# Branch steps ahead of the weight unit on ScalarE and VectorE in the token mixers of a two-layer encoder

## The chip, the cores and the metric

The kernel runs on one core of one Trainium2 chip. The metric is the device time of one execution in microseconds (us). The kernel before was timed three times; the figure that stands for it is the median, 1176.68 us.

## What is computed

The reference is a hybrid encoder trunk with two layers over 256 tokens of width 1024. Cut to what matters here:

```python
for l in range(DEPTH):                      # 2 layers
    xn = rms_norm(h, norm_mix_g[l])
    q, k, v, u_f, u_x, u_g, gates = split(xn @ w_in[l] + b_in[l])   # 1024 x 6144
    y_a = neighbourhood_attention(q, k, v, rpb[l])       # 8 heads of 64
    y_b = fourier_mix(u_f)                               # real part of a 2-D DFT
    y_c = recurrent_branch(u_x, u_g, ...)                # conv, forward and backward RG-LRU, GeLU gate
    merged = sum(sigmoid(gates_k) * (y_k @ w_branch[l, k]) for k in (a, b, c))
    h = h + merged @ w_out[l]
    xn = rms_norm(h, norm_ffn_g[l])
    h = h + (swiglu(xn, ...) if l % 2 == 0 else moe_swiglu(xn, ...))  # dense, then top-2 of 8 experts
return rms_norm(h, final_g)
```

All matrix products with weights are done to float32 accuracy: each operand is split into a high part in fp32r and the rest, and three products (high x high, high x rest, rest x high) are added up.

## The kernel before

Weights come as **units** of 128 x 1024 floats (512 KB). One unit passes through four hands. SyncE's queue loads it into a ring of six raw buffers (`load`, line 289). ScalarE copies it to its high part (`hi`, line 456), VectorE takes the difference (`lo`, line 758), and TensorE multiplies with both (lines 1245 to 1247). The split halves live in a ring of RH = 4 buffers, so ScalarE and VectorE work AHEAD = 3 units ahead: in turn k of a mixer they prepare unit k + 3 while TensorE is at unit k. `hi` of unit u waits until the load has landed and until TensorE has used unit u - 4, which is the moment TensorE begins turn u - 3. `lo` waits for `hi`; TensorE waits for `lo`; a load waits for the `lo` that frees its raw buffer.

A mixer has U_MIX = 68 turns: 48 for the input projection (12 groups of four units, in the order u_f, u_x, q, k, v, u_g and six for the gates), 12 for the branch projections and 8 for the output projection. The order of work on each engine is written out by hand: a loop over k with, in each turn, the branch steps due in it. TensorE does its small branch matmuls at the head of a turn, then the unit's 24 matmuls of 256 columns, or 12 of 512.

The steps that matter below, with the turn in which they stand:

- Turn 4 and 5 of layer 0: VectorE `set_up_columns` (lines 798 to 806, signals `col_ok`), ScalarE takes an absolute value and an exponential from it (lines 499 and 500, signal `lam_act`), VectorE `set_up_decay` (lines 812 to 825).
- Every fourth turn: the group that has just ended is evacuated from PSUM (lines 512, 518, 524 on ScalarE; 854, 860, 867 on VectorE).
- Turn 8: first Fourier matmuls (1332), copies (531, 894). Turns 9 to 12: the four taps of the convolution (883, 885). Turn 12: second Fourier matmuls (1341), copies and the mirror (902 to 910, signal `yb_full`). Turn 13: ScalarE makes the high part of y_b (535, `yb_h`). Turn 14: VectorE its low part (914, `yb_l`).
- Turn 16 and 25: TensorE's gate matmuls of the forward and the backward scan (1358). The first of them waits for `yb_l`. Activations 545, 555, 563, 571 and VectorE's 953 to 974 follow through turns 16 to 33; the scans are 971 and 974.
- Turns 28 to 48, every even one: attention, two heads on 128 queries at a time, j = 0 to 7. TensorE makes scores (1374; it waits for the row maximum of j - 1), the product with V of j - 3 (1386; it waits for `pt_ok`, and at each new pair of heads for `ya_l`) and transposes of j - 2 (1397). VectorE adds the bias and finds the maximum (930 to 933, `s_max`) and normalises j - 1 (937, 939). ScalarE copies the transposes (585) and takes the exponential (590). `ya_h` (596) and `ya_l` (945) split an output.
- Turns 34 to 41: the GeLU gate (981 to 995; 574, 577 on ScalarE).

GpSimd only adds the column mask to the attention's bias tables (418), four times in a mixer, as the tables land.

Of the kernel before, what the change touches and what calls it, by code (L numbers as in the profile page):

```python
# [42 lines left out]
AHEAD = RH - 1  # L43
# [9 lines left out]
U_MIX = U_IN + U_BR + U_OUT  # L53
# [50 lines left out]
def build(nc, x, norm_mix_g, w_in, b_in, rpb, conv_w, conv_b, lru_wa, lru_ba, lru_wx, lru_bx,  # L104
# [12 lines left out]
    with ExitStack() as ctx:  # L117
# [150 lines left out]
        def place(u):  # L268

            if u < BASE_MOE:  # L270
                return raw[:, u % RAW, :], raw_full[u % RAW], 16 * (u // RAW + 1)
            turn, j = (u - BASE_MOE) // RAW_MOE, (u - BASE_MOE) % RAW_MOE
            if j < RAW:
                return raw[:, (BASE_MOE + j) % RAW, :], raw_full[(BASE_MOE + j) % RAW], 16 * ((BASE_MOE + j) // RAW + turn + 1)
            return mix[:, UNIT * (j - RAW):UNIT * (j - RAW + 1)], mix_full[j - RAW], 16 * (turn + 1)
# [164 lines left out]
        def _(act):  # L440
# [7 lines left out]
            def hi(base, k, i=0, per=0):  # L448

                u = base + k  # L450
                ring = RAW_MOE if u >= BASE_MOE else RAW
                src, arrived, count = place(u)
                act.wait_ge(arrived, 16 * (per // ring) * i + count)
                if u >= RH:
                    act.wait_ge(unit_used, i * per + (u - RH + 1))
                act.activation(w_hi[:, u % RH, :], src, ACT.Copy).then_inc(hi_done, 1)  # L456
# [22 lines left out]
            def mixer(l):  # L479
                B = BASE_MIX[l]  # L480
# [10 lines left out]
                    norm(2 * l)  # L491
                    norm_hi(2 * l)
                for k in range(U_MIX):
                    if k + AHEAD < U_MIX:
                        hi(B, k + AHEAD)
                    if l == 0 and k == 4:

                        act.wait_ge(col_ok, 1)
# [98 lines left out]
                    for dg in range(2):  # L597
                        if k == U_IN + 6 * (dg + 1) + 1:
                            for b in range(2):
                                act.wait_ge(merged, 4 * l + 2 * dg + b + 1)  # L600
                                at = 1024 * dg + 512 * b
                                act.activation(xhf[:, at:at + 512], gflat[:, at:at + 512],
                                               ACT.Copy, scale=0.5).then_inc(mh_ok, 1)

            def step_hi(n, dst, i=0, per=0):

                for b in range(2):
                    act.wait_ge(prod_ok, 2 * i * per + (2 * n - 1 + b))
                    act.activation(dst[:, 512 * b:512 * b + 512], prod_t[:, 512 * b:512 * b + 512],
                                   ACT.Copy).then_inc(ah_ok, 1)  # L610
# [33 lines left out]
            def experts(p):  # L644
# [85 lines left out]
                rows_hi((E + 1) * (p + 1), 0)  # L730

            mixer(0)
            dense()
            mixer(1)
            norm(3)
            experts(0)
# [8 lines left out]
        def _(dve):  # L745
# [8 lines left out]
            def lo(base, k, i=0, per=0):  # L754

                u = base + k
                dve.wait_ge(hi_done, i * per + (u + 1))
                dve.tensor_tensor(w_lo[:, u % RH, :], place(u)[0],  # L758
                                  w_hi[:, u % RH, :].bitcast(F32), ALU.subtract).then_inc(lo_done, 1)
# [67 lines left out]
            def mixer(l):  # L827
                B = BASE_MIX[l]
# [5 lines left out]
                if l == 0:  # L834
                    lo(B, 2)
                for k in range(U_MIX):
                    if k + AHEAD < U_MIX:
                        lo(B, k + AHEAD)
                    if l == 0 and k == 4:
                        set_up_columns()  # L840
                    if l == 0 and k == 5:
# [180 lines left out]
                    for dg in range(2):  # L1022
                        if k == U_IN + 6 * (dg + 1) + 1:
                            for b in range(2):
                                dve.wait_ge(mh_ok, 4 * l + 2 * dg + b + 1)
                                at = 1024 * dg + 512 * b
                                dve.scalar_tensor_tensor(out=xlf[:, at:at + 512], in0=gflat[:, at:at + 512], scalar=0.5,
                                                         in1=xhf[:, at:at + 512].bitcast(F32), op0=ALU.mult,
                                                         op1=ALU.subtract).then_inc(ml_ok, 1)

                if l == 0:
                    for k in range(AHEAD):
# [193 lines left out]

            dve.memset(eps_t[:, :], EPS).then_inc(eps_ok, 1)
            mixer(0)
            dense()
            mixer(1)  # L1230
            norm(3)
            experts(0)
# [400 lines left out]
```

## Time and profile before

| | before |
|---|---|
| three timed runs | 1176.68, 1180.18, 1175.78 us |
| median | 1176.68 us |
| the profiled execution's own time | 1180.34 us |
| its span, first to last instruction | 1178.5 us |
| TensorE matmuls busy | 1133.8 us (96%) |
| VectorE busy | 879.0 us (75%) |
| ScalarE busy | 721.2 us (61%) |
| mean granted TensorE clock | 0.991 |

The profiled execution took 0.31% longer than the median; its span leaves out 1.84 us around it. The layer 0 mixer lies from about 15 to 246 us of the span, the dense feed-forward to 454 us, the layer 1 mixer from 464 to 688 us, and the experts after it. TensorE is busy almost throughout, and VectorE is full only in the experts' part, which the change does not touch. So the profile is to be read for TensorE's waits inside the mixers, not for shares of the span.

### The profile page before, as it was taken

The numbers are of one execution on the slowest core, as the hardware profiler recorded it, in microseconds if no ns is written. First come the engines' busy times: TensorE is split into PE (matmuls) and PEld (weight loads), VectorE is DVE, ScalarE is ACT, GpSimd is POOL, SyncE is SP. The second block draws the span as 40 slices with busy tenths as digits, with TensorE's granted clock in tenths as the row PEclk, the third lists the DMA queues.
The fourth block names the chain that finished last, engine by engine and source line by source line (L and its number), as shares of the span: only waits on it lengthen the run. The fifth ranks groups of instructions, "written<-read, shape, count | busy, mean of one in ns | idle before, by whom it ended". The sixth has DMA issues, their size and how long they took to land.

```text
span 1178.5 us, 19502 instructions
## 1 busy us (share of the span) xinstructions
PE 1133.8 (96%) x7004; PEld 994.2 (84%) x7004; DVE 879.0 (75%) x1049; ACT 721.2 (61%) x941; POOL 23.8 (2%) x21
## 2 busy tenths in 40 slices
PE   7989999989999998999999989999999999999995
PEld 6979889979999997989889958888888888888883
DVE  4956885854544466666885869999999999999985
ACT  4447764445444345357764457777777878777774
POOL 0300000000000000200000000000000000000000
PEclk9989999999999999999999999999999999999998
DMA  9945445555655667745445398999999999999940
GB/s 280 255 138 180 125 143 179 168 172 181 192 169 165 204 199 190 209 152 179 126 144 178 109 339 298 342 323 347 331 333 337 327 337 322 350 318 352 325 165 38
DMA packets 137897, 271.70 MB, mean 231 GB/s; under 512 B 26424, under 2 KB 26736, under 8 KB 137840
## 3 DMA queue, kind: packets, MB, share of 16 engines
q1 hardware_dynamic: 136832, 267.26, 69.5%
q0 software_dynamic: 1008, 3.67, 1.0%
q8 instruction: 37, 0.61, 0.2%
q14 instruction: 20, 0.16, 0.0%
HBM read 269.84 MB, written 1.05 MB: 230 GB/s over the span
## 4 chain that ended last, share of the span: by engine, by line
PE 85%; DVE 9%; ACT 3%; issue 2%; DMA 1%; DVEq 0%; ACTq 0%; POOLq 0%
PE ps L1245 26%; PE ps L1247 25%; PE ps L1246 25%; DVE w_lo L758 4%; DVE h L1124 2%; PE ps L1358 1%; ACT w_hi L456 1%; PE ps L1306 1%; PE ps L1491 1%; PE ps L1492 1%; PE ps L1471 1%; DMA row<-in_norm_mix_g_dram 1%; PE ps L1470 1%; PE ps L1386 1%; PE ps L1397 1%
## 5 line engine op out<-in xcount | busy, mean ns | idle before, releaser
L758 DVE TENSOR_TENSOR w_lo<-raw,w_hi 128x1024 fp32r<-128x1024 f32 x304 | 372.5, 1239 | 198.8 <-ACT w_hi L456 193.8
L456 ACT ACTIVATE w_hi<-raw 128x1024 fp32r<-128x1024 f32 x304 | 317.8, 1058 | 256.4 <-PE ps L1247 244.4
L1245 PE MATMUL ps<-xh,w_hi 128*128 128x256 f32 x1024 | 292.8, 286 | 0.1
L1247 PE MATMUL ps<-xh,w_lo 128*128 128x256 f32 x1024 | 290.1, 283 | 0.0
L1246 PE MATMUL ps<-xl,w_hi 128*128 128x256 f32 x1024 | 290.1, 283 | 0.0
L758 DVE TENSOR_TENSOR w_lo<-mix,w_hi 128x1024 fp32r<-128x1024 f32 x192 | 230.7, 1222 | 29.1 <-ACT w_hi L456 24.0
L456 ACT ACTIVATE w_hi<-mix 128x1024 fp32r<-128x1024 f32 x192 | 203.7, 1061 | 72.1 <-PE ps L1247 72.0
L1245 PE MATMUL ps<-w_hi,xh 128*128 128x512 f32 x512 | 203.7, 398 | 0.8 <-issue 0.2
L1247 PE MATMUL ps<-w_hi,xl 128*128 128x512 f32 x512 | 199.9, 390 | 0.0
L1246 PE MATMUL ps<-w_lo,xh 128*128 128x512 f32 x512 | 199.7, 390 | 0.0
L1245 PEld LDWEIGHTS ps<-xh,w_hi 128*128 128x128 f32 x1024 | 196.7, 192 | 3.0 <-issue 2.1
L1246 PEld LDWEIGHTS ps<-xl,w_hi 128*128 128x128 f32 x1024 | 196.7, 192 | 0.3
L1247 PEld LDWEIGHTS ps<-xh,w_lo 128*128 128x128 f32 x1024 | 196.5, 192 | 0.0
L1245 PEld LDWEIGHTS ps<-w_hi,xh 128*128 128x128 f32 x512 | 96.3, 188 | 26.3 <-DVE w_lo L758 5.9
L1245 PE MATMUL ps<-w_hi,yh 128*128 128x512 f32 x288 | 115.4, 401 | 0.8 <-DVE yl L1100 0.2
L1247 PEld LDWEIGHTS ps<-w_hi,xl 128*128 128x128 f32 x512 | 96.2, 188 | 20.7
L1247 PE MATMUL ps<-w_hi,yl 128*128 128x512 f32 x288 | 112.6, 391 | 0.0
L1246 PE MATMUL ps<-w_lo,yh 128*128 128x512 f32 x288 | 112.4, 390 | 0.0
L1246 PEld LDWEIGHTS ps<-w_lo,xh 128*128 128x128 f32 x512 | 96.5, 188 | 18.8
L1245 PEld LDWEIGHTS ps<-w_hi,yh 128*128 128x128 f32 x288 | 54.2, 188 | 14.2 <-issue 4.1
L1247 PEld LDWEIGHTS ps<-w_hi,yl 128*128 128x128 f32 x288 | 54.1, 188 | 11.7
L1246 PEld LDWEIGHTS ps<-w_lo,yh 128*128 128x128 f32 x288 | 54.2, 188 | 10.1
(202 smaller groups left out, 1121.8 us busy)
## 6 DMA issues: line engine op xcount, KB each, us to landing
mix<-in_moe_w_gu_dram SPq DMA_DIRECT2D x112, 512.0 KB, 5.3
raw<-in_w_in_dram SPq DMA_DIRECT2D x96, 512.0 KB, 4.1
raw<-in_moe_w_gu_dram SPq DMA_DIRECT2D x80, 512.0 KB, 5.7
mix<-in_moe_w_down_dram SPq DMA_DIRECT2D x80, 512.0 KB, 4.6
raw<-in_ffn_w_gu_dram SPq DMA_DIRECT2D x48, 512.0 KB, 3.9
raw<-in_w_branch_dram SPq DMA_DIRECT2D x24, 512.0 KB, 3.4
raw<-in_ffn_w_down_dram SPq DMA_DIRECT2D x24, 512.0 KB, 4.9
raw<-in_w_out_dram SPq DMA_DIRECT2D x16, 512.0 KB, 3.4
```

The costliest lines, as they stand in the source:

```text
L456: act.activation(w_hi[:, u % RH, :], src, ACT.Copy).then_inc(hi_done, 1)
L758: dve.tensor_tensor(w_lo[:, u % RH, :], place(u)[0], w_hi[:, u % RH, :].bitcast(F32), ALU.subtract).then_inc(lo_done, 1)
L1124: dve.tensor_tensor(h[:, t, 512 * half:512 * half + 512], ps[:, (6, 7, 4, 5)[q], :], h[:, t, 512 * half:512 * half + 512], ALU.add).then_i ...
L1245: mm(dst, ah, bh, start=first, stop=False, skip_group_check=True)
L1246: mm(dst, ah, bl, start=False, stop=False, skip_group_check=True)
L1247: return mm(dst, al, bh, start=False, stop=last, skip_group_check=True)
L1306: ins = pe.transpose(ps[:, 4 + c // 2, at:at + P], hn[:, t, P * c:P * c + P], ident)
L1358: ins = mm(ps[q, 4 + 2 * g + m // 2, SEQ * (m % 2):SEQ * (m % 2) + SEQ], wlru[q, d, g, m, :], conv_t[q, m, :], start=True, stop=True)
L1386: ins = mm(ps[HD * hh:HD * hh + HD, 6, P * t:P * t + P], v_t[:, kt, HD * hd:HD * hd + HD], pt_t[:, hh, P * kt:P * kt + P], start=(kt == 0) ...
L1397: ins = pe.transpose(ps[:, 7, at:at + P], p_t[:, j % 2, hh, P * kt:P * kt + P], ident)
L1470: mm(ps[:, 6 + half, :], g_t[:, t, :], yhf[:, o:o + 512], start=(t == 0), stop=False)
L1471: ins = mm(ps[:, 6 + half, :], g_t[:, t, :], ylf[:, o:o + 512], start=False, stop=(t == TT - 1))
```

## The change

In both mixer loops the call that prepares unit k + 3 moves from the head of turn k to its tail, on ScalarE and on VectorE. Nothing else moves; TensorE's, GpSimd's and SyncE's programs are the same.

```diff
@@ ScalarE, mixer(l)
                 for k in range(U_MIX):
-                    if k + AHEAD < U_MIX:
-                        hi(B, k + AHEAD)
                     if l == 0 and k == 4:
...
                                 act.activation(xhf[:, at:at + 512], gflat[:, at:at + 512],
                                                ACT.Copy, scale=0.5).then_inc(mh_ok, 1)
+                    if k + AHEAD < U_MIX:
+                        hi(B, k + AHEAD)
@@ VectorE, mixer(l)
                 for k in range(U_MIX):
-                    if k + AHEAD < U_MIX:
-                        lo(B, k + AHEAD)
                     if l == 0 and k == 4:
                         set_up_columns()
...
                                                          op1=ALU.subtract).then_inc(ml_ok, 1)
+                    if k + AHEAD < U_MIX:
+                        lo(B, k + AHEAD)
```

## Rows read from the trace of the kernel before

**Rows 1.** Waits of TensorE, whole span: total us, times, longest us

```profile
PE ps L1306 <- DVE gates L769: 13.0, 5, 3.5
PE ps L1358 <- DVE yl L914: 3.7, 1, 3.7
PE ps L1386 <- DVE yl L945: 2.5, 2, 1.2
PE ps L1374 <- DVE small L933: 2.0, 2, 1.0
```

**Rows 2.** Windows: length, busy us of PE, PEld, DVE, ACT, POOL, clock, DMA

```profile
66.00:68.00 2.00, 0.12 (x2) 0.00 (x0) 1.07 (x2) 2.00 (x3) 0.00 (x0) 1.00 0.23 28
...
70.00:72.00 2.00, 2.00 (x12) 1.03 (x12) 2.00 (x3) 0.00 (x0) 0.00 (x0) 0.50 0.74 224
...
150.00:152.00 2.00, 1.15 (x8) 0.55 (x7) 1.22 (x6) 1.56 (x6) 0.00 (x0) 1.00 0.76 213
```

**Rows 3.** Timeline of TensorE, layer 0: start, length, what, [idle before]

```profile
37.70 3.62 PE L1332 MATMUL ps<-cst,mix 128*128 128x256 f32 x16
...
69.79 6.41 PE L1358 MATMUL ps<-mix,wlru 64*64 64x256 f32 x32 [3.67 <-DVE yl L914]
...
101.65 3.67 PE L1358 MATMUL ps<-mix,wlru 64*64 64x256 f32 x32
...
142.82 0.70 PE L1374 MATMUL ps<-mix 64*128 64x256 f32 x4 [1.00 <-DVE small L933]
...
152.40 0.66 PE L1386 MATMUL ps<-pt_t,mix 128*64 128x128 f32 x8 [1.24 <-DVE yl L945]
```

**Rows 4.** Timeline of ScalarE, 28 to 68 us

```profile
33.91 1.99 ACT L456 ACTIVATE w_hi<-raw 128x1024 fp32r<-128x1024 f32 x2
...
47.16 1.06 ACT L456 ACTIVATE w_hi<-raw 128x1024 fp32r<-128x1024 f32 x1 [1.82 <-PE ps L1247]
50.04 1.06 ACT L456 ACTIVATE w_hi<-raw 128x1024 fp32r<-128x1024 f32 x1 [1.82 <-PE ps L1247]
...
65.34 1.06 ACT L535 ACTIVATE yh<-mix 128x1024 fp32r<-128x1024 f32 x1 [6.70 <-DVE mix L910]
66.31 2.93 ACT L456 ACTIVATE w_hi<-raw 128x1024 fp32r<-128x1024 f32 x3
```

**Rows 5.** Timeline of VectorE, 27 to 70 us

```profile
27.48 1.23 DVE L758 TENSOR_TENSOR w_lo<-raw,w_hi 128x1024 fp32r<-128x1024 f32 x1 [1.51 <-ACT w_hi L456]
...
31.22 0.25 DVE L798 COPY col<-ps 128x96 f32<-128x96 f32 x1
...
34.98 1.23 DVE L758 TENSOR_TENSOR w_lo<-raw,w_hi 128x1024 fp32r<-128x1024 f32 x1 [1.57 <-ACT w_hi L456]
36.12 1.83 DVE L812 TENSOR_SCALAR small<-small 128x16 f32<-128x16 f32 x1
...
41.16 5.15 DVE L758 TENSOR_TENSOR w_lo<-raw,w_hi 128x1024 fp32r<-128x1024 f32 x3
...
52.30 3.30 DVE L885 SCALAR_TENSOR_TENSOR mix<-mix,col 128x256 f32<-128x256 f32 x4
...
56.78 1.66 DVE L885 SCALAR_TENSOR_TENSOR mix<-mix,col 128x256 f32<-128x256 f32 x4
...
64.62 0.69 DVE L910 TENSOR_TENSOR mix<-mix 128x508 f32<-128x508 f32 x1
```

**Rows 6.** Timeline of GpSimd, layer 0, the last of its four mask steps

```profile
53.09 1.84 POOL L418 TENSOR_TENSOR mix<-mix,cst 128x768 f32<-128x768 f32 x1 [4.35 <-DMA mix<-in_na_rpb_dram]
```

**Rows 7.** Timeline of SyncE's queue: the load of unit 14

```profile
40.40 1.81 SPq L289 DMA_DIRECT2D raw<-in_w_in_dram  x1
```

**Rows 8.** Timeline of VectorE in the attention, layer 0

```profile
136.70 1.22 DVE L758 TENSOR_TENSOR w_lo<-raw,w_hi 128x1024 fp32r<-128x1024 f32 x1 [0.60 <-ACT w_hi L456]
137.84 2.28 DVE L971 TENSOR_TENSOR_SCAN mix<-mix 128x1024 f32<-128x1024 f32 x1
...
151.83 0.42 DVE L945 TENSOR_TENSOR yl<-ps,yh 128x256 fp32r<-128x256 f32 x1 [0.71 <-ACT yh L596]
```

## The prediction, made before the changed kernel was run

> **What bounds the kernel now.** I read TensorE's waits first, because its busy share is 96% and only a wait of its own can be shortened by an order. The largest group, 13.0 us for line 1306, belongs to the norms, which the change leaves alone. Inside the mixers stand three kinds: 3.67 us before the first gate matmuls (line 1358, waiting for VectorE's `yb_l`), once; 1.0 us before the scores (line 1374, waiting for the row maximum), once in each mixer; 1.24 us before the product with V (line 1386, waiting for `ya_l`), once in each mixer [rows 1, 3]. Everything else in the mixers is TensorE at work: ScalarE's `hi` waits for TensorE at 47.16 and 50.04, so a unit costs 2.88 us [rows 4].
>
> Then the windows, for the clock. In the 3.67 us wait the granted clock is still 1.00 in 66 to 68 us and 0.50, that is 1.2 GHz, in 70 to 72 [rows 2]. The same 32 gate matmuls take 6.41 us there and 3.67 us for the backward scan [rows 3], so the wait costs another 2.8 us by the clock (6.35 against 3.60 us to the next unit; I take 2.8). In the 1.24 us wait the window shows 1.00, that is 2.4 GHz [rows 2]. All that the change can win is 3.67 + 2.8 + 2 x (1.0 + 1.24) = 10.95 us.
>
> Last the timelines of ScalarE and VectorE ahead of each wait: is the engine idle, or busy with something that could stand behind?
>
> **Part 1, turns 4 to 16 of layer 0.** VectorE is full without a gap from 34.98, where it starts `lo` of unit 8, to 65.31, where `yb_full` is signalled (64.62 + 0.69) [rows 5]. Those 30.33 us hold `lo` of units 8 to 15, eight of them, and the steps of turns 5 to 12. With the steps first they hold `lo` of units 7 to 14, again eight, and the same steps. So the end moves by as much as the start does.
>
> The start: after the change VectorE goes on from `lo` of unit 6 (27.48, free at about 28.62) straight to `set_up_columns` instead of waiting for `hi` of unit 7. From its first copy at 31.22 to ScalarE's next `hi` at 33.91 are 2.69 us (columns, one table load, two small activations) [rows 4, 5]. Hence `hi` of unit 7 starts at 28.62 + 2.69 = 31.3, `lo` of unit 7 at 32.4. VectorE's full stretch runs from 32.4 to 32.4 + 30.3 = 62.7.
>
> Is TensorE fed meanwhile? Its first Fourier matmuls start at 37.70 and take 3.3 us to the next unit [rows 3], so turn 7 starts at 37.7 - 2.9 = 34.8 and unit 8 at 41.0. `lo` of unit 7 ends at 33.6, 1.2 us early. `set_up_decay` takes 41.16 - 36.12 = 5.0 us, from 33.5 to 38.6, and `lo` of unit 8 ends at 39.8, 1.2 us early too. Behind it the cover grows: three `lo` in 5.15 us [rows 5] against 2.88 us for a unit. SyncE's queue loses nothing: the load of unit 14 waits for `lo` of unit 8 (39.8) and was issued at 40.40 anyway, behind its table loads [rows 7]; those of units 15 and 16 wait for `lo` of 9 and 10, which come earlier than now (41 and 43.7 against 42.4 and 46.3). GpSimd's mask steps hang on the tables alone.
>
> Unit 15 is where it costs. TensorE ends unit 15 at 69.79 - 3.67 = 66.12, so it wants it at 66.12 - 2.88 = 63.2 [rows 3, 4]. Its `lo` now stands behind the twelfth turn's tap, copies and mirror: 62.7 + 1.2 = 63.9. A new wait of 0.7 us; unit 15 ends at 66.8. Queued behind that `lo` are `lo` of unit 16 and then `yb_l`.
>
> The chain to the gate matmuls: `yb_full` at 62.7; ScalarE's high part 1.06 and, ahead of `yb_l` in both engines' order, `hi` of unit 16: 0.97 to its start [rows 4] and 1.06, so 64.8; `lo` of unit 16 1.14 to the next start; `yb_l` 1.22 like every 1024-wide one: 67.2. The gate matmuls start at 67.25 instead of 69.79, a gain of 2.5 us. TensorE then stood for 0.7 and, with a unit between, 0.4 us. Both are shorter than the 1.24 us under which the clock held, so I take the full clock and 2.8 us more. Sum of part 1: 5.3 us. Layer 1 has no set-up; there `yb_l` is no wait now (rows 1 have line 1358 once), and its chain has more room than here, so I cost that at nothing; the price if this cover fails is the same 0.7.
>
> The bounds. GpSimd's mask steps hold VectorE up: four taps of line 885 beside one took 3.30 us, alone 1.66 [rows 5, 6]. There are four such collisions in the stretch, and I assumed that they cost the same in the new order; one more or one less full collision moves `yb_full` by 1.6 us, and with it the gain. The Trainium skill's page SBUF — State Buffer, section Who interferes with whom, says that a VectorE instruction with two SBUF inputs contends with a GpSimd instruction that reads SBUF, and one with a single input outside the two-port modes does not; by that rule a mask step that falls on copies out of PSUM costs VectorE nothing, and the sum would be better by up to the same 1.6. The trace agrees in the 3.30 against 1.66. The other bound is the clock: if the two short waits bring 1.2 GHz, 2.8 us go back. Part 1 lies between 5.3 - 1.6 - 2.8 = 0.9 and all of it, 6.5 us.
>
> **Part 2, attention, both mixers.** The cause of both waits is one backlog on VectorE around the scan of turn 33. It is now: `lo` of unit 36, waited for 0.60 us and begun at 136.70, scan at 137.84, `lo` of unit 37, maximum of j = 3 at 142.8, and so on until `ya_l` at 151.83 [rows 8]. In the new order the scan stands behind `lo` of unit 35 alone, and the maximum behind `lo` of unit 36. I followed the turns from 25 on by the durations of the timeline (`lo` 1.14 from start to start, maximum 1.61, normalise 0.7, exponentials 1.0, `hi` 1.06, each table load 1.28). ScalarE is then the later one in turn 32 (table load, gates, transposes' copy, exponentials and only then `hi` of unit 35, ending at 134.9). `lo` of unit 35 runs at 134.9, the scan at 136.0 instead of 137.84, the maximum is there at 141.0, TensorE wants it at 141.8: the 1.0 us wait is gone. The next: `ya_l` starts at 150.05 instead of 151.83. TensorE's product starts at 150.6 instead of 152.40. What is late next is still `ya_l`, by 0.5 us. So the gain is 1.8 us in each mixer, 3.6 in all. It can't pass 2.24 each, and if ScalarE's `hi` of unit 35 is so late that only the one `lo` is saved, it is 1.1.
>
> What the moved `lo` leave to TensorE there: unit 37 is ready at 144.7 and wanted at 146.4, units 39, 41 and 43 are 1.7 to 2.5 us early, all others more. The branch projections need nothing: with the 3.9 us of adding up first, `lo` of unit 63 is ready at 228.8 for 231.7.
>
> **Sum.** 5.3 + 3.6 = 8.9 us of 1180.34, so 1171.4 for the profiled execution, and against the median 1176.68 - 8.9 = 1167.8 us. All later work, dense and experts, moves up unchanged.
>
> **The rivals.**
> A: the clock falls all the same in turns 15 and 16. For: it had fallen within the 3.67 us of waiting; two waits in 5 us are new. Against: 1.00 through the 1.24 us wait, which follows the 1.0 us one by 8.6 us. Gain 8.9 - 2.8 = 6.1, time 1170.6.
> B: the change doesn't do what it says: VectorE's work in front of `yb_l` and of the maximum is nearly the same sum in either order, other orders of the semaphores and collisions eat the lead of 2.6 us (34.98 - 32.4), and `yb_l` comes under 1 us earlier, with the clock at 1.2 GHz; in the attention 1.1 us each. Gain about 1 + 2.2 = 3.2, time 1173.5. For: VectorE has no gap there. Against: the lead comes from a gap of 1.57 us before 34.98 [rows 5], which is real.
> C, slower: TensorE starves for weights in the attention. In an even turn `hi` of unit k + 3 now waits for scores, maximum and exponentials, 0.7 + 1.6 + 1.0, and then 1.06 + 1.22 until `lo`; three units of 2.88 cover that, but VectorE is over 3 us in arrears after the scan. It decides when VectorE is over 1.7 us later than I followed it at unit 37. If three even turns in each mixer then stand 1.6 us and the clock falls once, each mixer loses 7.6 us instead of winning 1.8: 1176.68 - 5.3 + 15.2 = 1186.6. Against: every margin I found is above 1 us.
>
> **How the numbers follow.** Forecast as told 0.60 (gain 6.5 to 10.9), A 0.15, B 0.18, C 0.07. The range goes from the forecast's best, 1176.7 - 10.9 = 1165.8, with half a microsecond for the median's own scatter 1165.3, up past A and into B, 1173.6. A measurement of this kernel can tell about 0.5% from no change, 5.9 us or 1170.8. The forecast lies beyond it, A about on the line, B within. Faster by over 0.5%: 0.60 + 0.08 = 0.68; within: 0.07 + 0.18 + 0.02 = 0.27; slower: 0.05.
>
> **What would show it.** Line 1358's wait under 1 us instead of 3.67, a new wait for `lo` (line 1245 on line 758) of 0.7 us one unit before, and the forward gate matmuls at 3.6 us with a clock of 1.00. The wait on line 933 gone in both mixers, that on line 945 about 0.5 instead of 1.24. `lo` of unit 7 at 32.4. It is wrong if TensorE waits for line 758 in several turns, if a clock of 0.50 stands after turn 15, or if the loads of units 10 to 16 land later than now.

## The result, and the profile after

The changed kernel took 1172.49 us (median of ten runs, 1170.74 to 1175.41) against 1179.9 us for the kernel before, timed beside it (ten runs, 1175.78 to 1184.49). The ratio is 0.9937, with a 95% interval of 0.9920 to 0.9954: faster by 7.4 us (5.4 to 9.4). Timed again later (g_after below) it was 0.9934 (0.9915 to 0.9953). In the profiled executions the span went from 1178.5 to 1169.5 us, 9.0 less. The forecast was 8.9 us less.

TensorE's waits after, as in [rows 1]: the waits on `yb_l` (3.7 us) and on the row maximum (2.0 us) are no longer in the list, that for `ya_l` (now line 943) is 0.7 us in each mixer.

```profile
PE ps L1306 <- DVE gates L769: 11.5, 4, 3.5
...
PE ps L1386 <- DVE yl L943: 1.4, 2, 0.7
```

TensorE's timeline after, at the places of [rows 3]. The gate matmuls start without a wait and last as long as the backward scan's did before; the scores of turn 36 wait for nothing.

```profile
36.98 3.62 PE L1332 MATMUL ps<-cst,mix 128*128 128x256 f32 x16
...
65.33 3.67 PE L1358 MATMUL ps<-mix,wlru 64*64 64x256 f32 x32
...
134.53 0.70 PE L1374 MATMUL ps<-mix 64*128 64x256 f32 x4
...
143.49 0.66 PE L1386 MATMUL ps<-pt_t,mix 128*64 128x128 f32 x8 [0.70 <-DVE yl L943]
```

The windows after, the last column but two being the granted clock (1.00 is 2.4 GHz, 0.50 is 1.2 GHz): it is at 2.4 GHz all through the forward gate matmuls, where it was at 1.2 in [rows 2].

```profile
66.00:68.00 2.00, 2.00 (x22) 1.28 (x20) 1.95 (x4) 0.28 (x1) 0.00 (x0) 1.00 0.80 241
68.00:70.00 2.00, 2.00 (x15) 1.29 (x12) 0.00 (x0) 0.95 (x3) 0.00 (x0) 1.00 0.84 293
```

VectorE's timeline after, for [rows 5] and [rows 8]:

```profile
25.55 1.23 DVE L758 TENSOR_TENSOR w_lo<-raw,w_hi 128x1024 fp32r<-128x1024 f32 x1 [1.20 <-ACT w_hi L456]
26.69 0.25 DVE L798 COPY col<-ps 128x96 f32<-128x96 f32 x1
...
30.46 1.23 DVE L758 TENSOR_TENSOR w_lo<-raw,w_hi 128x1024 fp32r<-128x1024 f32 x1 [1.57 <-ACT w_hi L456]
...
36.53 3.49 DVE L758 TENSOR_TENSOR w_lo<-raw,w_hi 128x1024 fp32r<-128x1024 f32 x3
39.94 0.87 DVE L865 TENSOR_SCALAR mix<-ps,col 128x256 f32<-128x256 f32 x2
40.73 0.74 DVE L892 COPY mix<-ps 128x256 f32<-128x256 f32 x2
42.28 1.23 DVE L758 TENSOR_TENSOR w_lo<-raw,w_hi 128x1024 fp32r<-128x1024 f32 x1 [0.81 <-ACT w_hi L456]
...
59.77 0.69 DVE L908 TENSOR_TENSOR mix<-mix 128x508 f32<-128x508 f32 x1
60.38 1.22 DVE L758 TENSOR_TENSOR w_lo<-raw,w_hi 128x1024 fp32r<-128x1024 f32 x1
62.53 1.23 DVE L758 TENSOR_TENSOR w_lo<-raw,w_hi 128x1024 fp32r<-128x1024 f32 x1 [0.94 <-ACT w_hi L456]
63.68 1.22 DVE L912 TENSOR_TENSOR yl<-mix,yh 128x1024 fp32r<-128x1024 f32 x1
...
127.79 1.23 DVE L758 TENSOR_TENSOR w_lo<-raw,w_hi 128x1024 fp32r<-128x1024 f32 x1 [0.61 <-ACT w_hi L456]
128.93 2.28 DVE L969 TENSOR_TENSOR_SCAN mix<-mix 128x1024 f32<-128x1024 f32 x1
```

To compare executions I take lengths between fixed points of TensorE, so that an earlier or later start drops out: stretch A from the first Fourier matmuls to the first unit after the forward gate matmuls, stretch B from the backward gate matmuls to the product with V of turn 40, both in layer 0.

| profile | A (us) | B (us) | `yb_full` after the start of A | wait on `yb_l` |
|---|---|---|---|---|
| before | 38.4 | 58.3 | 27.6 | 3.67 |
| changed | 32.0 | 56.6 | 23.5 | none |
| changed, second profile | 32.4 | 56.6 | 24.3 | 0.2 |

The 9.0 us of the spans are made up so: the first Fourier matmuls already start 0.7 us earlier (36.98 against 37.70), ahead of any place where the order could reach TensorE; A gives 6.5; B gives 1.7; the rest of layer 0, the dense part and layer 1 up to the router give 1.1, less than the 1.0 + 1.24 - 0.7 = 1.5 us by which the two waits of layer 1's attention shrank; the experts give 0.2; and the last scatter with what follows it takes 1.2 back. That last piece is clock. TensorE waits 2.22 us before it in both kernels. In the profile of the kernel before the clock stayed at 2.4 GHz (first row), in that of the changed kernel it fell (the next two):

```profile
1164.00:1166.00 2.00, 1.48 (x6) 1.24 (x7) 1.18 (x3) 1.11 (x2) 0.00 (x0) 1.00 0.02 4
```

```profile
1154.00:1156.00 2.00, 1.70 (x4) 1.42 (x5) 0.74 (x2) 0.89 (x2) 0.00 (x0) 0.60 0.00 0
1156.00:1158.00 2.00, 1.99 (x5) 1.03 (x4) 1.58 (x3) 0.00 (x0) 0.00 (x0) 0.55 0.04 8
```

### The profile page after: what moved, and what is told of

It is laid out like the page before. It is cut to its first block, busy times and chain, and to the rows that moved or that the text cites. A ratio compares the mean times of both kernels' runs of the same rounds, so it can differ in the third digit from the quotient of the medians.

```text
span 1169.5 us, 19502 instructions
## 1 busy us (share of the span) xinstructions
PE 1133.6 (97%) x7004; PEld 996.7 (85%) x7004; DVE 877.4 (75%) x1049; ACT 720.5 (62%) x941; POOL 24.9 (2%) x21
## 3 DMA queue, kind: packets, MB, share of 16 engines
q0 software_dynamic: 1008, 3.67, 0.9%
## 4 chain that ended last, share of the span: by engine, by line
PE 82%; DVE 9%; ACT 5%; issue 3%; DMA 1%; DVEq 0%; ACTq 0%; POOLq 0%
PE ps L1245 25%; PE ps L1247 24%; PE ps L1246 24%; DVE w_lo L758 4%; ACT w_hi L456 2%; DVE h L1124 2%; PE ps L1358 1%; PE ps L1306 1%; PE ps L1491 1%; PE ps L1492 1%; PE ps L1471 1%; PE ps L1470 1%; PE ps L1386 1%; PE ps L1332 1%; PE ps L1481 1%
```

## The experiments

Each edit is told against the kernel before unless it says otherwise. Every ratio is to the kernel before, run beside it. e_setup and e_rest were executed once each, for their profiles, and have no ratio. In the fences line numbers are those of each experiment's own file, and differ by up to four from those before.

### Which half of the mixer gives what: f_front and f_late

```diff
@@ f_front, both engines (hi on ScalarE, lo on VectorE)
-                    if k + AHEAD < U_MIX:
+                    if k + AHEAD < U_MIX and not (k < 25):
                         lo(B, k + AHEAD)
...
+                    if k + AHEAD < U_MIX and (k < 25):
+                        lo(B, k + AHEAD)
@@ f_late: the same with k >= 25
```

> Both units moved to the tail in turns 0 to 24 only, in both mixers. Own theory: TensorE's 3.67 us wait before the gate matmuls is gone, they take 3.6 us at a clock of 1.00, and the attention's waits stay at 1.0 and 1.24 us in each mixer. Gain 6.5 us of about 1179, ratio 0.9945. Rival (the wait went because the first loads landed earlier in the profile of the changed kernel, by 1.2 us against TensorE, not because of the order): part of the wait, 1 to 2 us, or a wait of TensorE for VectorE's low half of unit 15 comes back, and the gain is 4 to 5 us.

Measured: ratio 0.9963 (0.9952 to 0.9974), 4.4 us. Its profile has no wait on `yb_l` nor for unit 15's low half, A is 32.0 and B 58.3 us: the early part of the change, and nothing else. The waits are as expected, but the timed gain is not: 6.5 us (ratio 0.9945) lies outside the interval. The last group of experiments comes back to this.

```profile
PE ps L1390 <- DVE yl L947: 2.5, 2, 1.2
...
PE ps L1378 <- DVE small L935: 2.0, 2, 1.0
```

> Both units moved to the tail from turn 25 on only, in both mixers. Own theory: the wait of 3.7 us before the first gate matmuls stays, with the clock at 1.2 GHz behind it and matmuls of 6.4 us; the wait on the row maximum is gone and that for the low half of y_a is 0.7 us, so 1.7 us gained in each mixer, 3.4 us in all, ratio 0.997. Rival (the two halves help each other, the backlog in the attention is carried over from turns 4 to 16): under 1 us in each mixer.

Measured: ratio 0.9983 (0.9966 to 1.0000), 2.0 us, where 3.4 were expected; the interval takes in both that and nothing. B is 56.6 us, as in the changed kernel, and both mixers have the 0.7 us wait alone. The early part is as before, and here the wait is 5.0 us where the profile of the kernel before had 3.67: the scatter of this wait between executions is over 1 us. Stretch A is 39.5 us.

```profile
PE ps L1362 <- DVE yl L916: 5.0, 1, 5.0
...
PE ps L1390 <- DVE yl L947: 1.4, 2, 0.7
```

What follows: each part takes away its own waits and leaves the other's alone, -6.4 and -1.7 us in the stretches of layer 0. The timed ratios multiply to 0.9946, which is the changed kernel's within its interval. The rival, that the wait went because the loads happened to land early, falls: f_front had less of a lead from the loads (VectorE's full stretch starts 5.55 us ahead of the first Fourier matmuls, 6.5 in the changed kernel) and starts its gate matmuls as early after them (28.4 us) as the changed kernel does (28.35).

### Which turns of the early part: e_setup and e_rest

```diff
@@ e_setup, both engines: the tail only in turns 4 and 5 of layer 0, the head elsewhere
+                    if k + AHEAD < U_MIX and (l == 0 and k in (4, 5)):
+                        lo(B, k + AHEAD)
@@ e_rest: the tail in turns 0 to 24 except those, the head elsewhere
+                    if k + AHEAD < U_MIX and (k < 25 and not (l == 0 and k in (4, 5))):
+                        lo(B, k + AHEAD)
```

> Both units moved to the tail in turns 4 and 5 of layer 0 alone. Own theory: VectorE's full stretch starts about 2.6 us earlier but holds one low half more, so yb_full comes 1.4 us earlier: TensorE's wait before the gate matmuls is 2.2 us instead of 3.67, with the clock falling or not. Rival (the set-up's place is of no account, the gain is from the low half behind turn 12's steps): the wait stays over 3.2 us.

> Both units moved to the tail in turns 0 to 24, but not in turns 4 and 5 of layer 0. Own theory: yb_full comes 1.1 us earlier only, and the low half of unit 15 stands behind it: TensorE waits about 2 us for that low half in turn 15 and 0.5 us more before the gate matmuls, 2.5 us in all. Rival (the place of turns 12 and 13 is the whole of it): no wait over 1 us.

Measured, e_setup: a wait of 1.94 us instead of 3.67, and the clock held, so A is 34.0 us.

```profile
67.05 3.67 PE L1362 MATMUL ps<-mix,wlru 64*64 64x256 f32 x32 [1.94 <-DVE yl L916]
```

e_rest: 2.49 us of waiting for the low half of unit 15 and 0.16 us more on `yb_l`, A is 34.9 us.

```profile
65.06 0.39 PE L1249 MATMUL ps<-xh,w_hi 128*128 128x256 f32 x1 [2.49 <-DVE w_lo L760]
68.35 3.67 PE L1362 MATMUL ps<-mix,wlru 64*64 64x256 f32 x32 [0.16 <-DVE yl L916]
```

The sums of the waits are as expected, within 0.3 us (1.94 for 2.2, 2.65 for 2.5). The early lead and the order in the other turns are both needed to take the wait away whole: with the lead alone (VectorE starts `set_up_columns` 9.7 us ahead of the first Fourier matmuls in e_setup, 6.5 before) 1.9 us are left, without it 2.65. Without the lead the moved low half itself becomes what TensorE waits for: the new wait that the forecast named is real, and in the changed kernel it is only just covered. In both profiles the clock stayed at 2.4 GHz.

### The clock's share: e_warm

```diff
                             if d:
                                 pe.wait_ge(lru_tanh, 2 * (2 * l + 1))
                             else:
+                                if l == 0:
+                                    for _ in range(16):
+                                        pe.transpose(ps[:, 7, 0:P], ident, ident)
                                 pe.wait_ge(yb_l, l + 1)
```

> The kernel before, with 16 transposes of the identity into a free PSUM bank put ahead of TensorE's wait for the low part of y_b in layer 0 (no result is changed, the bank is overwritten). Own theory: the wait itself stays, filled with about 3.4 us of transposes, but the clock stays at 2.4 GHz and the 32 gate matmuls take 3.6 instead of 6.4 us: gain 2.8 us, ratio 0.9976. Rival (transposes don't keep the clock up, or the matmuls are slow there for another reason): 6.4 us again and no gain.

Measured: ratio 0.9982 (0.9969 to 0.9996), 2.1 us. The transposes took 1.91 us, not 3.4, so 1.41 us of waiting is left behind them; the clock was 1.00 throughout and the matmuls took 3.67 us. A is 35.2 us, 3.2 less than in the profile before, of which 0.4 is a wait shorter by scatter.

```profile
66.97 1.91 PE L1353 MATMUL ps<-cst 128*128 128x128 f32 x16
70.29 3.67 PE L1361 MATMUL ps<-mix,wlru 64*64 64x256 f32 x32 [1.41 <-DVE yl L914]
```

In its ten timed runs the mean clock was 0.991 to 0.994, in the thirteen of the kernel before beside them 0.986 to 0.992. So the 2.8 us are the clock's, and they can be had without touching the order.

### What made VectorE late: e_mask

```diff
@@ GpSimd, mask_tables
                 pool.wait_ge(bias_in[hp], 16 * 4 * (l + 1))
+                pool.wait_ge(lru_ps, 2 * l + 1)
```

> The kernel before, with GpSimd's four mask steps held back until the forward gate matmuls, so that they no longer run beside VectorE's turns 5 to 12. Own theory: the four collisions cost VectorE about 5.9 us there; without them yb_l is in time, TensorE's wait before the gate matmuls is 0 and they take 3.6 us: gain 6.5 us, ratio 0.9945, without any move of the units. Rival (VectorE is held by waits for ScalarE and the loads, the collisions only fill these): the wait stays over 2 us.

Measured: ratio 0.9937 (0.9917 to 0.9957), 7.4 us; A is 31.95 us and TensorE waits for nothing in it. In the old order of units, `yb_full` comes 23.2 us after the start of A (61.18 against 37.97), 4.4 us sooner than before. Of these, 3.5 are VectorE's full stretch, 26.85 us long instead of 30.33; the other 0.9 is its earlier start, scatter of the loads. That is less than the 5.9 us expected, because VectorE now stands 1.86 and 0.43 us for ScalarE's `hi` inside the stretch, where it had no gap before. The attention's waits are as before. The mask steps that ran beside VectorE are thus a cause of the wait as good as the order of the units: taking away either removes it.

```profile
45.65 1.23 DVE L759 TENSOR_TENSOR w_lo<-raw,w_hi 128x1024 fp32r<-128x1024 f32 x1 [1.86 <-ACT w_hi L457]
```

The collisions are moved, not gone. The four mask steps now run in turns 16 to 19, ahead of the attention, and the two low halves beside them take 5.41 us instead of 2.35; nothing waits for these.

```profile
70.19 8.26 POOL L419 TENSOR_TENSOR mix<-mix,cst 128x768 f32<-128x768 f32 x4 [57.01 <-PE ps L1359]
74.12 5.41 DVE L759 TENSOR_TENSOR w_lo<-raw,w_hi 128x1024 fp32r<-128x1024 f32 x2 [4.54 <-ACT w_hi L457]
```

### One engine's half: f_dveonly

```diff
@@ VectorE, mixer(l); ScalarE is left as before
-                    if k + AHEAD < U_MIX:
-                        lo(B, k + AHEAD)
...
+                    if k + AHEAD < U_MIX:
+                        lo(B, k + AHEAD)
```

> Only VectorE's half of the change: its low half stands at the tail, ScalarE's high half stays at the head of the turn. Own theory: what counts is what stands ahead of the steps on VectorE; ScalarE's high half at the head even spares the low half its wait (unit 16 behind the high part of y_b, unit 35 behind the exponentials). All waits of the change go, and the 0.7 us for the low half of y_a too: gain 10 to 11.5 us, ratio 0.991. Rival (ScalarE's order matters as much, since maximum, exponential and split of y_a pass through it): the waits of 1.2 us for the low half of y_a come back in each mixer, gain 8 us or less.

Measured: ratio 0.9902 (0.9883 to 0.9921), 11.6 us; the lowest ratio of all, in four runs, its interval touching that of the changed kernel. No wait of TensorE in the mixers is left, neither on `yb_l` nor in the attention: A is 31.95, B 55.85 us. VectorE's `ya_l` starts 45.8 us after the backward gate matmuls (142.37 against 96.57), 50.2 before and 48.5 in the changed kernel. The scan follows its `lo` without VectorE having stood for ScalarE in front of either:

```profile
127.23 1.23 DVE L758 TENSOR_TENSOR w_lo<-raw,w_hi 128x1024 fp32r<-128x1024 f32 x1
128.38 2.28 DVE L969 TENSOR_TENSOR_SCAN mix<-mix 128x1024 f32<-128x1024 f32 x1
```

In the changed kernel VectorE stands for a high half 0.81 us at 42.28, 0.94 at 62.53 and 0.61 at 127.79, just ahead of the scan (fence above). Only the first of these is new. The other two were in the kernel before as well, one unit later: 0.60 us at 136.70 [rows 8], and

```profile
67.38 1.23 DVE L758 TENSOR_TENSOR w_lo<-raw,w_hi 128x1024 fp32r<-128x1024 f32 x1 [0.93 <-ACT w_hi L456]
```

At both places `hi` and `lo` of a unit stand at the same end of a turn, before at the head and after at the tail, and `lo` comes straight behind `hi` and waits for it. With `hi` at the head and `lo` at the tail, ScalarE is ahead by the steps of a turn, and these two waits go. ScalarE's move kept them and gave nothing in return. ScalarE's half alone wasn't tried: by the program, VectorE's `lo` of unit 7 at the head of turn 4 would wait for a `hi` behind ScalarE's step of that turn, which waits for VectorE's `set_up_columns` behind that `lo`.

### The last wait of the attention: f_yaearly

```diff
@@ changed kernel, ScalarE: high part of y_a ahead of the exponentials
+                    if j >= 4 and j % 2 == 0 and j - 3 < NA:
+                        ...
+                        act.activation(yh[:, hp, :], ps[:, 6, 0:SEQ], ACT.Copy).then_inc(ya_h, 1)
                     if 0 <= j < NA:
                         act.wait_ge(s_max, NA * l + j + 1)
```

> The changed kernel, with ScalarE's high part of y_a (which needs only the product that TensorE did ahead of the transposes) moved ahead of the same turn's exponentials. Own theory: it ends 1 us earlier, VectorE's low part starts when VectorE is free, 0.7 us earlier, and TensorE's last wait in the attention falls from 0.7 to 0.1 us at most: 1.2 us better than the changed kernel, ratio to the kernel before 0.9925. Rival: VectorE, not ScalarE, is what comes last there; the wait stays at 0.7 us.

Measured: ratio 0.9912 (0.9893 to 0.9932), 10.4 us. The 0.7 us wait is gone in both mixers and B is 55.85 us, 0.76 less than in the changed kernel. ScalarE's exponentials were what stood ahead of it. In this execution the wait on `yb_l` was 0.17 us and A 32.2 us: the cover there is thin.

### Is the rest of the timed gain lost to a thin margin: g_after, g_frontmask, g_dvemask

The stretches that the change touches are shorter by about 9.7 us, and the timed gain was 7.4. The changed kernel again (g_after) and two combinations of the edits above, f_front with e_mask (g_frontmask) and f_dveonly with e_mask (g_dvemask), were run beside each other.

> The changed kernel once more, unaltered, beside the two that follow. Stage by stage its profile was 9.9 us shorter than before in the places that the change touches, but the timed runs gave 7.4 (5.4 to 9.4). Theory M (margins: in some executions the loads land so that part of the wait ahead of the gate matmuls comes back): ratio again about 0.994, and this profile may show a wait of up to 1 us there. Rival S (plain scatter of the timed runs): ratio 0.9916, 9.9 us.

> Both units at the tail in turns 0 to 24 only, and GpSimd's four mask steps held back until the forward gate matmuls. That gives VectorE up to 5 us more room ahead of them. Theory M: with the margin the full 6.4 us show in the timed runs, ratio 0.9946, where the same without the mask's move gave 0.9963. Rival S: no wait is left in either, so the ratio stays at 0.9963 within 0.0005.

> VectorE's low half at the tail of every turn, ScalarE's high half at the head, and GpSimd's mask steps held back until the forward gate matmuls. No wait of TensorE inside the mixers in any execution. Both theories: at least as fast as VectorE's half alone, ratio 0.990; theory M up to 0.5 us better where a margin was short there, the rival the same within 0.5 us.

Measured: g_after 0.9934 (0.9915 to 0.9953), g_frontmask 0.9963 (0.9947 to 0.9979), g_dvemask 0.9917 (0.9898 to 0.9936). g_frontmask is where f_front was, although `yb_full` came 3 us sooner (20.85 us after the start of A, 23.9 in f_front): the theory of margins falls for the timed gain. Plain scatter is not borne out either: the changed kernel came out at 0.9937 and again at 0.9934, though 0.9916 lies just inside the second interval. The second profile of the changed kernel does show the margin in small: a wait of 0.2 us on `yb_l` and A longer by 0.5. The late mask steps add nothing to VectorE's half alone. The six runs of g_dvemask (1169.43 to 1171.11 us) all lie below the six of g_after (1171.33 to 1172.98), beside which they ran: that `lo` at the tail is better with `hi` left at the head is seen here most clearly.

What the profiles offer in its place is the clock behind the norms' waits. In f_front the clock fell in the norm after the first mixer and stayed at 1.2 GHz for over 6 us, into the dense units; in the kernel before it was back inside the norm. From the backward gate matmuls of layer 0 to the forward ones of layer 1 f_front took 1.6 us more than the kernel before (414.96 against 413.35), at the same waits in the attention and the norms. The five other profiles with the old order in the attention took 413.07 to 413.41. The second profile of the changed kernel took 0.8 us more there than its first (412.36 against 411.52). First the kernel before, then f_front:

```profile
249.00:251.00 2.00, 2.00 (x11) 1.61 (x12) 1.96 (x4) 0.30 (x1) 0.00 (x0) 0.62 0.02 7
251.00:253.00 2.00, 1.87 (x9) 1.47 (x9) 1.25 (x3) 1.76 (x4) 0.53 (x1) 0.53 0.12 43
253.00:255.00 2.00, 2.00 (x19) 2.00 (x19) 2.00 (x4) 1.25 (x2) 0.00 (x0) 1.00 0.69 217
```

```profile
244.00:246.00 2.00, 1.87 (x9) 1.46 (x8) 1.25 (x3) 1.63 (x4) 0.53 (x1) 0.50 0.09 18
246.00:248.00 2.00, 2.00 (x10) 2.00 (x11) 2.00 (x4) 1.37 (x2) 0.00 (x0) 0.50 0.71 240
248.00:250.00 2.00, 2.00 (x12) 2.00 (x11) 0.63 (x1) 0.00 (x0) 0.00 (x0) 0.50 0.21 27
```

That the time goes with the clock is seen in the kernel before: of its 44 runs beside the experiments, the four with a mean clock of 0.994 took 1176.4 us on average, the nine with 0.986 took 1182.1. The mean clock was 0.989 to 0.991 in all sixteen runs of the changed kernel and 0.992 to 0.994 in the four of f_dveonly; 0.002 of 1170 us are 4.7 us at half the clock, or 2.3 us lost, which would be the missing part. But in g_dvemask it was 0.989 to 0.992, hardly above the changed kernel's. That the norms are where the timed runs lose their 2 us is therefore not shown, and why one order should meet the low clock more often stays open.

## Why the prediction was right, and where it was off

**The bound.** TensorE's waits inside the mixers were the whole of it, as read; all that could be won was put at 10.95 us, and the variant that removes every one of them (f_dveonly) gained 11.6 (9.3 to 13.8). Layer 1 has no wait on line 1358 after the change, as taken.

**The lead.** The forecast had VectorE's full stretch start 5.3 us ahead of the first Fourier matmuls, from the 2.69 us of the set-up chain. It was 6.5 in the changed kernel (30.46 against 36.98), 5.1 in its second profile, 5.6 in f_front and 5.4 in f_yaearly. The step holds; the 1.2 us more in the first is scatter of the loads, since `hi` of unit 6 also came that much earlier against TensorE.

**The length of the stretch** is the term that was mis-sized: 30.3 us assumed; measured 30.0 in the changed kernel and 29.5 in its second profile, in f_front and in f_yaearly. I kept all four collisions with GpSimd, and counted them as equal; before, they cost 1.66, 1.66, 0.92 and 1.64 us, 5.9 in all. In the new order the second mask step (39.54, 2.20 us long) fell on lines 865 and 892, whose source is PSUM, and these took 0.87 and 0.74 us as without one.

```profile
39.54 2.20 POOL L418 TENSOR_TENSOR mix<-mix,cst 128x768 f32<-128x768 f32 x1 [3.44 <-DMA mix<-in_na_rpb_dram]
44.49 2.01 POOL L418 TENSOR_TENSOR mix<-mix,cst 128x768 f32<-128x768 f32 x1 [2.75 <-DMA mix<-in_na_rpb_dram]
```

By the rule quoted from the Trainium skill, SBUF — State Buffer, section Who interferes with whom, an instruction with at most one SBUF input, outside the two-port modes, does not contend with GpSimd; the trace agrees in these two. The sum had priced this collision like the others. The other three collisions cost 1.56, 1.52 and 1.61 us, 4.7 in all. Against this 1.2 us stands the 0.81 in which VectorE waited for `hi` of unit 11, which I had taken as covered: ScalarE's `hi` stood behind the copies of the Fourier result.

**The new wait for unit 15's low half**, 0.7 us by the forecast, was not there: it ended at 61.60 for a TensorE that wanted it at 62.4. With 0.3 us less in the stretch and 1.2 us more lead the two agree. The longer lead was luck of this execution, but the wait stayed away without it: in f_front, f_yaearly and the second profile, with leads of 5.1 to 5.6 us, the low half was 0.3 to 0.5 us early, because the stretch was 0.8 shorter. e_rest shows the wait at 2.49 us when the lead is missing.

**From `yb_full` to `yb_l`** the forecast had 4.5 us (62.7 to 67.2, with its end at the start of the matmuls); it took 64.90 - 60.46 = 4.4. Right.

**The clock** held, as taken, and its price was 2.8 us; e_warm shows it alone. Part 1 so came to 6.5 us, its upper bound, instead of 5.3 (6.0 in the second profile).

**Part 2** was put at 1.8 us in each mixer with 0.5 us of waiting left; it was 1.7 and 0.7. The scan started 1.8 us earlier by the forecast; against the backward gate matmuls it was 34.5 instead of 36.2 us, 1.7. The cause and the next in line, `ya_l`, were right.

**What it left out** is the scatter of the clock at the waits that the change does not touch: 1.2 us at the last scatter, and 0.8 to 1.6 over the two norms between the mixers (from gate to gate 411.52 and 412.36 us in the two profiles of the changed kernel, 413.35 in the kernel before and 414.96 in f_front).

**The number.** The mechanism was right; that the profiled execution met the forecast to 0.1 us (1171.27 for 1171.4) was luck. Stretch A gave 1.2 us more than part 1 and TensorE reached it 0.7 earlier for no reason of the order; the two attentions gave 0.4 less than part 2, the rest up to the experts' end 0.2 less, and the last scatter took 1.2 back. The timed gain, 7.4 us (5.4 to 9.4), fits the forecast's 8.9 and rival A's 6.1 alike: only the traces tell them apart. The forecast time, 1167.8 us, was 4.7 too low, and 3.2 of these came from the figure it started from, 1176.68 us as the median of three runs, where ten gave 1179.9.

**The rivals.** A, the clock falls in turns 15 and 16: no, but the changed kernel had no two waits there to try it; e_rest had 2.49 and 0.16 us, and the clock was at 1.00. (The 1.24 us wait follows the 1.0 us one by 8.3 us, not 8.6.) B, the lead is eaten up: no. C, TensorE starves in the attention: no wait on line 758 there; the place where it does starve when the lead is missing is turn 15. The list left out the variant that proved best, that only VectorE's order matters.

## What to carry to other kernels

In a pair of engines that prepare weights ahead of a third, ask which one is full there (VectorE, from 34.98 to 65.31 us, although it is busy for only 75% of the span): putting the urgent steps first pays on the full engine, while the one with room (ScalarE) is better left ahead, so that the full one never waits for it. Before moving work, look for what runs beside the late engine on another one: four GpSimd steps that could run 30 us later without harm cost as much as the order of the units. A wait of TensorE is to be counted twice where the profile shows the granted clock at 1.2 GHz behind it: once for itself and once for the matmuls that run slower (3.67 and 2.8 us here).

## What the runs showed of the hardware that was not expected

The clock did not fall in the same wait each time. With 1.94 us of waiting (e_setup) and with 2.49 us (e_rest) it stayed at 2.4 GHz; before the last scatter, at 2.22 us, it stayed in the kernel before and fell in the changed one; with 3.67 and 5.0 us it fell. In the norm ahead of the router, where TensorE waits 2.6 and then 0.2 us, it held in six of the thirteen profiles and fell in seven. In the two norms between the mixers, at 3.5 us of waiting, it fell in all thirteen. Once down it came back some 3 us after TensorE had taken up work again (norm after the first mixer in the changed kernel, work from 240.07, clock 1.00 again in 244 to 246 and 0.74 on average in 242 to 244) or only after more than 7 us (the same norm in f_front, work from 242.12, 0.50 still in 248 to 250).

A GpSimd step on SBUF held up small VectorE steps as much as large ones. Line 812, 128 x 16 from one SBUF input, took 1.83 us beside a mask step [rows 5] and 0.17 in the changed kernel, where none ran beside it; line 820, of the same size with more SBUF inputs, took 1.73 us in the changed kernel beside one and 0.17 before.

The same wait of TensorE, in the same order of work, was 3.67 us in one execution and 5.0 in another (f_late), and the first Fourier matmuls, behind the first eight units, started between 36.7 and 39.1 us over the thirteen profiles.
